# Expert row blocks loaded by quarters of features and turned on VectorE

## The reference, cut to what matters

```
def moe_ffn(h, w_router, router_bias, w_gate, w_up, w_down):
    ...
    _, idx = lax.top_k(masked, TOP_K)
    w = jnp.take_along_axis(scores, idx, axis=-1)
    w = w / jnp.sum(w, axis=-1, keepdims=True)
    gates = ...
    a = jnp.einsum('bld,edf->blef', h, w_gate)
    u = jnp.einsum('bld,edf->blef', h, w_up)
    return jnp.einsum('blef,efd->bld', jax.nn.silu(a) * u * gates[..., None], w_down)
```

## Time and profile before

| | |
|---|---|
| median of 3 runs | 1084.48 us (1083.26 to 1086.16) |
| span of the profiled execution, first to last instruction | 1080.7 us |
| outside the span, for the median | 3.8 us |
| PE busy / DVE busy / ACT busy | 920.4 / 349.6 / 295.9 us |
| experts of layer 0, first row load to last store | 490.96 to about 647 us |
| experts of layer 1, the same | 898.47 to about 1055 us |

### The profile page before, as it was taken

One profiled execution on the slowest core, in us unless ns is written; L12 is line 12 of the kernel. 1 busy time (PEld: TensorE's weight loads), 2 busy tenths in 40 slices (PEclk: granted clock), 3 DMA queues, 4 the chain that ended last, 5 costly groups with the idle time before them and its releaser, 6 DMA issues.

```text
span 1080.7 us, 14047 instructions
## 1 busy us (share of the span) xinstructions
PE 920.4 (85%) x5603; PEld 491.9 (46%) x5603; DVE 349.6 (32%) x909; ACT 295.9 (27%) x696; POOL 85.2 (8%) x96
## 2 busy tenths in 40 slices
PE   4999988777888889966999987997999965999994
PEld 1455645554644545543332326654545542333324
DVE  0422005645548640040110113474663140110112
ACT  2311023243345640041210112223673051110210
POOL 2400000101100001040000001000000141000002
PEclk9899998977889899967999997997899977999997
DMA  9999999843377202236899978014000326799925
GB/s 386 427 425 387 374 378 415 326 173 124 117 278 281 106 1 76 101 120 230 350 424 423 425 306 330 20 62 182 1 1 1 115 95 258 317 427 416 418 106 186
DMA packets 36339, 258.98 MB, mean 240 GB/s; under 512 B 3408, under 2 KB 3552, under 8 KB 21424
## 3 DMA queue, kind: packets, MB, share of 16 engines
q1 hardware_dynamic: 20448, 198.27, 45.6%
q0 software_dynamic: 12224, 47.01, 11.6%
q10 hardware_dynamic: 3600, 12.78, 2.9%
HBM read 236.73 MB, written 54.87 MB: 270 GB/s over the span
## 4 chain that ended last, share of the span: by engine, by line
PE 70%; DVE 9%; DMA 7%; ACT 7%; issue 4%; POOL 1%; PEld 1%; SPq 0%; DVEq 0%; POOLq 0%; ACTq 0%; PEldq 0%
PE ps L494 21%; PE ps L655 13%; PE ps L677 8%; PE ps L902 6%; DMA U<-expert_rows 3%; PE ps L508 3%; PE ps L639 3%; PE ps L457 2%; PE ps L731 2%; DMA ring<-w_in 2%; PE ps L533 2%; PE ps L515 2%; ACT hT L1046 1%; DMA expert_rows<-U 1%; ACT U L1026 1%
## 5 line engine op out<-in xcount | busy, mean ns | idle before, releaser
L655 PE MATMUL ps<-ring,U 128*32 128x512 f32 x1200 | 166.3, 592 | 0.0
L494 PE MATMUL ps<-U,ring 128*128 128x384 f32 x320 | 106.4, 489 | 2.7 <-DVE U L1465 1.4
L655 PEld LDWEIGHTS ps<-ring,U 128*32 128x32 f32 x1200 | 47.5, 110 | 85.3 <-issue 85.3
L677 PE MATMUL ps<-ring,U 128*32 128x512 f32 x672 | 85.7, 594 | 0.0
L494 PEld LDWEIGHTS ps<-U,ring 128*128 128x128 f32 x320 | 59.6, 189 | 46.9 <-issue 5.0
L655 PE MATMUL ps<-U 128*32 128x512 f32 x168 | 73.1, 592 | 0.0
L655 PE MATMUL ps<-hT,U 128*32 128x512 f32 x168 | 73.1, 592 | 0.0
L457 PE MATMUL ps<-ring,cond_w 128*32 128x384 f32 x512 | 59.6, 592 | 15.8 <-ACT cond_w L958 8.7
L902 PE MATMUL ps<-ring,hT 128*128 128x384 f32 x192 | 63.2, 488 | 1.7 <-issue 0.9
L639 PE MATMUL ps<-small,U 128*128 128x128 f32 x192 | 31.8, 319 | 38.4 <-DMA U<-expert_rows 36.1
L494 PE MATMUL ps<-hT,ring 128*128 128x384 f32 x192 | 63.3, 488 | 0.9 <-issue 0.8
(11 more groups left out here) (295 smaller groups left out, 1309.6 us busy)
## 6 DMA issues: line engine op xcount, KB each, us to landing
ring<-w_in SPq DMA_DIRECT2D x102, 1536.0 KB, 11.0
expert_rows<-w_in POOLq DMA_DIRECT2D x16, 2048.0 KB, 86.3
U<-expert_rows SPq DMA_DIRECT2D x24, 512.0 KB, 6.4
expert_rows<-U ACTq DMA_DIRECT2D x24, 512.0 KB, 9.1
hT<-w_in SPq DMA_DIRECT2D x6, 1536.0 KB, 12.1
U<-w_in SPq DMA_DIRECT2D x6, 1536.0 KB, 15.5
small<-small_in SPq DMA_DIRECT2D x1, 3147.5 KB, 37.2
xT<-x_in SPq DMA_DIRECT2D x1, 1536.0 KB, 16.8
```

What stands on the lines that cost most here:

```text
L494: ins = mm(out, lhs(k), rhs(k), start=(k == 0), stop=(k == n - 1))
L655: ins = mm(ps[q:q + 32, r, :], xgT[:, r, P * k + q:P * k + q + 32], w[e][:, c:c + 512], start=(k == 0), stop=(k == DC - 1))
L677: ins = mm(ps[q:q + 32, 6 + h, :], actT_of[i % NR][:, P * j + q:P * j + q + 32], w[e][:, c:c + 512], start=(j == 0), stop=(j == 1))
```

## The change

The rows are scattered with their features in another order: a feature 128 k + 32 s + j, with s from 0 to 3 and j from 0 to 31, is put at 256 s + 32 k + j of the row. A block comes in four DMAs, one for each s: 32 partitions get 256 features of 32 rows, for each of the four experts in turn. VectorE then turns the whole block, 128 x 1024, by one instruction that turns each 32 x 32 square in its place. After that a partition holds one feature of each chunk k, and the 32 columns at 256 e + 32 k are the rows of expert e. TensorE's row turns, the two PSUM banks that they used, and both copies go. VectorE waits for the load itself, and for the `up` products that still read the old `xgT`.

```
                     if g:
-                        sp.wait_ge(S["turned1"], N_BLOCK * l + i - NR + 1)
-                    sp.dma_start(xgb[r], block_of(rows_d, i)).then_inc(xg_full[r], 16)
+                        sp.wait_ge(S["xgT_ready"], N_BLOCK * l + i - NR + 1)
+                    for s in range(4):
+                        sp.dma_start(xgb[r][32 * s:32 * s + 32, :].rearrange("p (q n) -> p q n", q=GS),
+                                     block_of(rows_d, i)[:, 256 * s:256 * s + 256].rearrange("(q p) n -> p q n", q=GS)).then_inc(xg_full[r], 16)
...
-                                pe.wait_ge(S["xgT_act"], n0 + NR * g + r + 1)
-                                pe.wait_ge(S["xgT_dve"], n0 + NR * g + r + 1)
+                                pe.wait_ge(S["xgT_ready"], n0 + NR * g + r + 1)
...
-                                ins = mm(ps[q:q + 32, r, :], xgT[:, r, P * k + q:P * k + q + 32], w[e][:, c:c + 512],
+                                ins = mm(ps[q:q + 32, r, :], xgT[:, r, 256 * e + 32 * k:256 * e + 32 * k + 32], w[e][:, c:c + 512],
...
-                for r in range(NR):
-                    turn_rows(r)
                 for g in range(NG):
                     i = NR * g
                     up(g)
-                    turn_rows(i + 3)
-                    turn_rows(i + 4)
                     turn_act(i)
                     turn_act(i + 1)
-                    turn_rows(i + 5)
                     down(i)
...
-                    emptied_by(act.copy(htok3[:, t, 512 * half:512 * half + 512], b[:, :]))
+                    emptied_by(act.copy(by_quarter(htok3[:, t, :])[:, 4 * half:4 * half + 4], b[:, :].rearrange("p (k s j) -> p k s j", k=4, s=4)))
...
-                    dve.wait_ge(S["turned1"], n0 + i + 1)
-                    dve.tensor_copy(xgT[:, i % NR, 512:1024], ps[:, 4, :]).then_inc(S["xgT_dve"], 1)
+                    dve.wait_ge(xg_full[i % NR], 64 * ((n0 + i) // NR + 1))
+                    if i >= NR:
+                        dve.wait_ge(S["up_done"], n0 + i - NR + 1)
+                    dve.transpose(xgT[:, i % NR, :], xgb[i % NR]).then_inc(S["xgT_ready"], 1)
...
                     product(i)
                     product(i + 1)
-                    turned_rows(i + 3)
                     product(i + 2)
-                    turned_rows(i + 4)
-                    turned_rows(i + 5)
-                    rows_out(i)
-                    rows_out(i + 1)
-                    rows_out(i + 2)
+                    for r in range(NR):
+                        turned_rows(i + NR + r)
+                        rows_out(i + r)
```

More of the change, by code:

```diff
@@ L178, in build @@
         xgT = xgT_a.rearrange("p (r n) -> p r n", r=NR)
+        by_quarter = lambda ap: ap.rearrange("p (s k j) -> p k s j", s=4, k=DC)
         xgb, ysb = [xgb0, xgb1, xgb2], [ysb0, ysb1]
@@ L212, in build @@
             row_copied qkv_ready rt_exp flags_ready chosen_ready rows_ready row_cleared scattered
-            turned0 turned1 xgT_act xgT_dve up_done sil_ready act_ready act_turned actT_ready down0 down1 y_act y_dve
+            xgT_ready up_done sil_ready act_ready act_turned actT_ready down0 down1 y_act y_dve
             diag_ready mixed_turned
@@ L223, in build @@
         y_picked = [[sem(f"y_picked{t}_{c}") for c in range(2)] for t in range(NT)]
-        beyond = "loaded turned xgT up sil act act_turned actT down y go stored".split()
+        beyond = "loaded xgT up sil act act_turned actT down y go stored".split()
         BEYOND = [{n: sem(f"beyond{l}_{n}") for n in beyond} for l in range(DEPTH)]
@@ L629, in moe @@
                 first = S_MOE1 if l else S_MOE0
[L631 to L640, removed]
                 def up(g):
@@ L701, in moe @@
                         for b in range(N_BEYOND):
[L702 to L706, removed]
+                            pe.wait_ge(B["loaded"], e * (96 * N_BEYOND) + 96 * (b + 1))
+                            pe.wait_ge(B["xgT"], e * N_BEYOND + (b + 1))
                             for k in range(DC):
                                 w = xgT_a[:, 512 * k:512 * k + 512] if k < 6 else htok[:, 512 * (k - 6):512 * (k - 6) + 512]
-                                ins = mm(ps[:, 0, :], xgb[1][:, P * k:P * k + P], w, start=(k == 0), stop=(k == DC - 1))
+                                for q in range(4):
+                                    ins = mm(ps[32 * q:32 * q + 32, 0, :], xgb[1][:, 256 * q + 32 * k:256 * q + 32 * k + 32], w,
+                                             start=(k == 0), stop=(k == DC - 1))
                             ins.then_inc(B["up"], 1)
@@ L1074, in moe @@
                 n0 = N_BLOCK * l
[L1076 to L1080, removed]
                 def silu(i):
@@ L1099, in store @@
                     act.dma_start(block_of(rows_d, i), ysb[i % 2]).then_inc(y_stored[i % 2], 16)
-                for r in range(NR):
-                    turned_rows(r)
                 for g in range(NG):
@@ L1124, in moe @@
                         for b in range(N_BEYOND):
-                            act.wait_ge(B["turned"], e * N_BEYOND + (b + 1))
-                            act.copy(xgb[1][:, 0:512], ps[:, 3, :]).then_inc(B["xgT"], 1)
                             act.wait_ge(B["up"], e * N_BEYOND + (b + 1))
@@ L1588, in moe @@
                         for b in range(N_BEYOND):
-                            dve.wait_ge(B["turned"], e * N_BEYOND + (b + 1))
-                            dve.tensor_copy(xgb[1][:, 512:1024], ps[:, 4, :]).then_inc(B["xgT"], 1)
+                            dve.wait_ge(B["loaded"], e * (96 * N_BEYOND) + 96 * (b + 1))
+                            dve.transpose(xgb[1], xgb[0]).then_inc(B["xgT"], 1)
                             dve.wait_ge(B["sil"], e * N_BEYOND + (b + 1))
@@ L1868, in moe @@
                             first = S_MOE1 if l else S_MOE0
-                            pool.dma_start(xgb[0], beyond_rows(rows_d, e, b)).then_inc(B["loaded"], 16)
+                            for s in range(4):
+                                pool.dma_start(xgb[0][32 * s:32 * s + 32, :].rearrange("p (q n) -> p q n", q=4),
+                                               beyond_rows(rows_d, e, b)[:, :, 256 * s:256 * s + 256].rearrange("r p n -> p r n")).then_inc(B["loaded"], 16)
                             for h, to in enumerate((xgT_a, htok)):
```

## The result

The changed kernel takes 1114.62 us (median of 4 runs, 1105.79 to 1121.78) against 1083.87 for the kernel before on the same chip: a ratio of 1.0297, 95% interval 1.0259 to 1.0335. It is slower, as forecast (1104), by half as much again: 31 us instead of 20. The profiled run is the quickest of the four, 1105.79 us with a span of 1104.2; it shows 23.5 us of the loss.

The account below looks back on a forecast made before the run. TensorE's instructions and the DMA queue were taken to bound the experts with almost the same period, the queue 3.3 us ahead; slower row loads add 10 us a layer, 20 on the 1080.7 span, 1100.7, plus 3.8 to the median: 1104 us, range 1077 to 1118.

Parts of the forecast that it names:

- The row loads decide, 2.5 us for a block: DMA queue: a block written 32 partitions at a time takes twice the time, 2.5 us instead of 1.24.
- The Trainium skill's rule on 32 partitions: Row loads: partitions 0 to 31 reach 8 of 16 ports, half the rate; a block would take an estimated 2.4 us.
- TensorE's 13.5 us a layer cannot be kept: Between `up` and `down`: dropped row turns free 13.5 us; at most 3.3 us plus the start's gain can be kept.
- 3.3 us of lead: End of layer 1: last weights land at 1031.0, `up` needs them at 1034.3; same number used for layer 0.
- The rival in which TensorE's time counts: Experts, both layers: the freed turns count in full, 13.5 x 2 = 27 us, 1057; chance 0.03.
- SP's twelve issues cost nothing: SP: 12 row loads instead of 3 take 5.1 us, 3.9 more, free while the DMA engines have work.
- bare 3.9 x 3 a layer: SP's row issues: their cost per layer if the DMA engines had no work meanwhile, 3.9 us x 3.
- The last weights land 11.3 + 2 us later: End of layer 1: nine slower blocks (11.3 us) and a 2 us later start move the landing from 1031.0 to 1044.3.
- The start: Start of a layer's experts: slower first loads and cold clock in `up` make it 2 us later in all.
- 10 us a layer in all: Experts: last weights land 10.0 us after `up` needed them before; two layers add 20 us to the span.
- TensorE waits at k = 0 or k = 6: `up` of groups 1 to 3: expected sign, waits for `w_in` there where the kernel before has none.
- A turn 1.23 us, copies behind it nothing, ScalarE's copy nothing: VectorE's turn 1.23 us; copies behind turns nothing, at most 2 us a group; ScalarE's copy into `htok` nothing.

Follow-up runs that it names:

- a_wide1k: Changed kernel with each row block loaded by four DMAs of 256 features over all 128 partitions, 1 KB pieces, feature rearrangement left out: 1095.24 us, ratio 1.0105.
- a_one: Changed kernel with each row block loaded by one DMA over 128 partitions in 4 KB pieces, feature rearrangement left out: 1077.1 us, ratio 0.9944.
- a_1k1: Changed kernel with one DMA per block over 128 partitions in 1 KB pieces (quarters of a row reversed), feature rearrangement left out: 1079.97 us, ratio 0.9963.
- a_twoq_same: Changed kernel with each block's quarters 0 and 2 issued by SP, 1 and 3 by ScalarE's queue: 1105.71 us, ratio 1.0227.
- a_mid: Changed kernel with SP's row loads of groups 1 to 3 behind the two weight slots that the group's k = 0 needs: 1114.34 us, ratio 1.0283.
- a_exp_act: Changed kernel with four DMAs per block, one expert's 32 rows each over 128 partitions, groups 1 to 3 issued by ScalarE's queue: 1246.78 us, ratio 1.1509.

## Why the prediction was right, and where its size was off

The direction and the mechanism held: TensorE's turns went, its time was spent waiting for weights, and the row loads at reduced rate set the period. Point by point:

- *The row loads decide, 2.5 us for a block.* Right. Against a_wide1k, which has the same issues and pieces at full width, the engine time rose by 27.1 us, 1.13 for each of 24 blocks; against a_one by 37.6, 1.57. I had 1.26. In time the width costs 10.1 and 8.1 us a layer against a_wide1k, all of it from k = 5 of group 1 on.
- *The Trainium skill's rule on 32 partitions* ("SBUF — State Buffer", section "Door 1: The DMA port swizzle") holds here, and somewhat more than half the rate is lost: 182 to 184 GB/s where row loads run, against 426 for weights. Its section "Can I just issue two DMAs to hit both halves?" says that two at once gain 6%. Here the queue's time for row loads is 530.0 - 492.8 + 24 x 1.24 (512 KB at 423 GB/s) = 67.0 us, and it falls by 11.3 us, 17%, with two queues on different halves, by 0.9 on the same half. A block is 2.8 us by this, where the estimate from the page was 2.4. The halves matter as the page has it. Its 6% is neither borne out nor refuted: this 17% is engine time, with weights beside the rows, and the layers got no shorter by it where the queue decides.
- *TensorE's 13.5 us a layer cannot be kept.* Right. With the load as before, a_one keeps 4.3 and 4.1 us of them, which is within the 3.3 us of lead plus what its start gains (2.0 and 0.9 us up to k = 5 of group 0). The rival in which TensorE's time counts is refuted by its waits for `w_in`.
- *SP's twelve issues cost nothing.* This is the step that failed. "It costs nothing as long as the DMA engines have work for 5.1 us, which the row loads themselves give at the price below." They don't give it after k = 5 of group 0, where the queue is empty: shares of 0.27 to 0.91 there in layer 0. Between a_1k1 and a_wide1k, one issue against four, lie 7.2 and 4.6 us a layer, 15 us in the ratio; that is about half of the bare 3.9 x 3 a layer that the text had named as its upper end. This is their price beside loads of full width. Up to k = 5 of group 1 the changed kernel takes no longer than a_wide1k (63.3 and 62.5 us against 63.1 and 63.7), so there the slow loads and the issues run side by side and don't add up; after it the issues cost nothing, as the prediction had it. In the changed kernel itself, halving SP's issues took 3 us a layer off, 8 us in the ratio, uncertain by some 6 (a_twoq_same), with the transfers as slow, though the second queue may have a share in that.
- *The last weights land 11.3 + 2 us later.* In the profile they land at about 1053.6, 120.2 us after 933.44; with the 1031.0 that I read before, it was 108.0 from 923.03. That is some 12 us later, where I had 11.3 from there. The number is near, but in part by luck: I had it as nine blocks of slower load, and it is six blocks of that and, ahead of them, a stretch in which the issues count too. The start cost 0.8 us instead of 2 (25.4 us from the first row issue to k = 5 of group 0, 24.6 before).
- *10 us a layer in all.* Measured 14.2 and 12.9. In the sum as it stands (2 for the start, 11.3 for the queue, less 3.3 of lead) the term that was most off is the lead: in layer 1 the start cost 0.8, the queue some 12, and of the lead nothing was spent. Adding one thing at a time, by the table, the steps are -4.2 for the turns, +3.3 for 1 KB pieces, +5.9 for the issues and +8.5 for the width (means of the two layers, each uncertain by a few us); since issues and slow loads don't add up everywhere, another order would share them out otherwise. In time by the ratios: -6, +2, +15 and +21 us, 32 in all.
- *TensorE waits at k = 0 or k = 6.* At k = 0 in all three groups. I had spent the 3.3 us of lead against the last landing; but TensorE already starts the last group late, by its wait ahead of k = 0, and cold (its last `up` of layer 1 takes 22.74 us instead of 20.64), and k = 6 of the last group comes 3.2 us after the landing, as before (that `up` ends at 1062.0, less 5.2 for k = 6 and 7, against 1053.6).
- *A turn 1.23 us, copies behind it nothing, ScalarE's copy nothing.* 1.24 us. The copies behind the turns stop `down` for 2.9 us in the whole run; in a_mid they decide. ScalarE's copy into `htok` takes 582 ns, as before.

## What to carry to other kernels

Where a transfer queue runs with nearly the period of the engine it feeds, an edit that frees the engine is worth only the queue's lead, and what it does to the transfers decides; compare GB/s at equal share. Cutting one load into four is two costs in two places: the width that each part writes counts where the queue is full, and the issues where it is dry; they need not add up. Behind a wait that is new to an engine, look for what stands behind it in that engine's order: it cost nothing with the rows first and ate a gain with the rows last.

## What was not expected of the hardware

An issue's time went with what it describes, and now and then one issue was held. At the start of a layer a 128 KB load into 32 partitions took SP 0.43 us. One that spreads 32 rows over 128 partitions took it 0.53 to 0.71 for the first six of layer 0 and 1.33 to 1.38 for the last six. In a_mid twelve of the former took 11.87 us behind weights, where they take 5.55 at the start:

```profile
557.38 11.87 SPq L389 DMA_DIRECT2D U<-expert_rows  x12
```

But eleven of them took 0.37 to 0.44 us each. One made the difference, as the 13.59 us did on ScalarE's queue in a_exp_act:

```profile
561.12 6.70 SPq L389 DMA_DIRECT2D U<-expert_rows  x1
```

Both times the DMA engines were busy with weights (share 1.0). What holds such an issue is not shown.
